# Making the low part of a streamed weight chunk two chunks ahead instead of three

## What is computed

```python
# block 1, two layers: modulated norms, FFN, attention, FFN
x = x + 0.5 * g1[:, None] * swiglu(h, ff_w13[l, 0], ff_w2[l, 0])
y = hybrid_conv_mla(...) if l % 2 == 0 else nsa_attention(...)
x = x + g2[:, None] * y
x = x + 0.5 * g3[:, None] * swiglu(h, ff_w13[l, 1], ff_w2[l, 1])
def swiglu(h, w13, w2):
    a, b = jnp.split(h @ w13, 2, axis=-1)
    return (jax.nn.silu(a) * b) @ w2
```

## Time and profile before

| | |
|---|---|
| Median of 3 runs | 3031.98 us (3030.12 to 3038.22) |
| The profiled execution | 3027.24 us |
| Its span, first to last instruction | 3025.4 us |
| Mean granted TensorE clock | 0.994 of full |
| TensorE busy | 2954.8 us, 98% |
| VectorE busy | 2338.3 us, 77% |
| ScalarE busy | 1727.1 us, 57% |
| GpSimd busy | 73.8 us, 2% |
| HBM | 243 GB/s over the span |

### The profile page before, as it was taken

The page is one execution under the profiler, slowest core; times in us unless marked ns, Lnnn a source line. Parts: engine busy times, 40 slices in busy tenths (PEclk is TensorE's granted clock), DMA queues, the critical chain, the costliest instruction groups (busy, mean ns, idle before and its releaser), DMA issues.

```text
span 3025.4 us, 56656 instructions
## 1 busy us (share of the span) xinstructions
PE 2954.8 (98%) x24887; PEld 2900.5 (96%) x24887; DVE 2338.3 (77%) x2648; ACT 1727.1 (57%) x1926; POOL 73.8 (2%) x143
## 2 busy tenths in 40 slices
PE   9999999999999999899999999999999999999999
PEld 8999999999989998899989999999999999899999
DVE  6897788888657567665777898898898898766776
ACT  5445454544535445444656777777777777545454
POOL 0110001010000000000000000000000000000000
PEclk9999999999999999999999999999999999999999
DMA  8885468687513653255416998998999899533352
GB/s 343 301 331 203 154 236 321 224 307 277 188 70 136 224 189 114 84 196 195 168 42 250 372 365 338 372 365 338 372 364 373 340 365 374 192 139 127 146 189 98
DMA packets 112412, 739.78 MB, mean 245 GB/s; under 512 B 12481, under 2 KB 12481, under 8 KB 32161
## 3 DMA queue, kind: packets, MB, share of 16 engines
q1 hardware_dynamic: 92304, 662.77, 58.4%
q0 software_dynamic: 19856, 73.34, 6.6%
HBM read 735.01 MB, written 1.05 MB: 243 GB/s over the span
## 4 chain that ended last, share of the span: by engine, by line
PE 84%; DVE 10%; ACT 4%; issue 1%; DMA 1%; SPq 0%; DVEq 0%; POOL 0%; ACTq 0%
PE ps L612 49%; PE ps L613 33%; DVE low L3079 3%; PE ps L627 2%; DVE AF L3061 2%; ACT whi L2081 2%; DVE att L3070 1%; DVE hl L3052 1%; DVE T L3052 1%; DVE gf L3064 1%; ACT cv L2066 0%; DVE T L3061 0%; DVE AF L3052 0%; DMA ring<-in_r 0%; ACT AF L2066 0%
## 5 line engine op out<-in xcount | busy, mean ns | idle before, releaser
L3079 DVE TENSOR_TENSOR low<-ring,whi 128x2048 fp32r<-128x2048 f32 x620 | 1414.3, 2290 | 369.9 <-ACT whi L2081 367.0
L2081 ACT ACTIVATE whi<-ring 128x2048 fp32r<-128x2048 f32 x620 | 1184.4, 1914 | 278.1 <-issue 173.6
L612 PE MATMUL ps<-whi,AR 128*128 128x256 f32 x5376 | 938.7, 278 | 0.0
L612 PEld LDWEIGHTS ps<-whi,AR 128*128 128x128 f32 x5376 | 819.0, 188 | 0.0
L612 PE MATMUL ps<-low,AR 128*128 128x256 f32 x2688 | 745.4, 277 | 0.0
L613 PE MATMUL ps<-hh,whi 128*128 128x256 f32 x2272 | 636.3, 280 | 0.2 <-DVE hl L3052 0.2
L613 PE MATMUL ps<-hl,whi 128*128 128x256 f32 x2272 | 629.1, 277 | 0.0
L613 PE MATMUL ps<-hh,low 128*128 128x256 f32 x2272 | 629.1, 277 | 0.0
L612 PEld LDWEIGHTS ps<-low,AR 128*128 128x128 f32 x2688 | 504.9, 188 | 0.0
L613 PEld LDWEIGHTS ps<-hh,whi 128*128 128x128 f32 x2272 | 426.1, 188 | 5.1 <-issue 1.0
L613 PEld LDWEIGHTS ps<-hl,whi 128*128 128x128 f32 x2272 | 426.0, 187 | 1.3 <-issue 1.0
(11 more groups left out here) (281 smaller groups left out, 3596.8 us busy)
## 6 DMA issues: line engine op xcount, KB each, us to landing
ring<-in_w SPq DMA_DIRECT2D x620, 1024.0 KB, 5.1
rring<-in_r POOLq DMA_DIRECT2D x135, 512.0 KB, 5.7
first<-in_r SPq DMA_DIRECT2D x8, 512.0 KB, 18.2
ring<-in_r SPq DMA_DIRECT2D x4, 512.0 KB, 8.6
rring<-in_r SPq DMA_DIRECT2D x3, 512.0 KB, 17.3
AF<-in_mem SPq DMA_DIRECT2D x1, 1024.0 KB, 8.4
X<-in_x SPq DMA_DIRECT2D x1, 1024.0 KB, 16.2
AF<-in_cst POOLq DMA_DIRECT2D x1, 1024.0 KB, 5.9
```

Source lines behind the costliest of these rows:

```text
L612: return self.e.matmul(out, l, r, start=start, stop=stop, skip_group_check=True)
L2081: self.e.activation(N.whi[:, c % HB, :], N.slot(c), ACT.Copy).then_inc(N.sem["hi"], 1)
L3079: self.e.tensor_tensor(N.wlo(c), N.slot(c), N.whi[:, c % HB, :].bitcast(F32), ALU.subtract).then_inc(N.sem["lo"], 1)
```

## The change

VectorE's `chunk()` makes lows up to two chunks ahead of its count instead of three. ScalarE's `chunk()` stays at three, as do the four places above that make lows with numbers of their own, and the number of buffers.

```diff
--- before.py
+++ after.py
@@ -3081,7 +3081,7 @@
             self.count.tick("lo", ())
 
     def chunk(self):
-        self.split_to(self.chunks + HB - 1)
+        self.split_to(self.chunks + HB - 2)
         self.chunks += 1
 
     def start(self):
```

## The result

Before 3031.74 us (median of 7 runs, 3026.75 to 3038.22), after 3041.90 us (7 runs, 3035.46 to 3044.78). The ratio of all runs is 1.0026, 95% interval 1.0013 to 1.0038: the change costs 7.9 us of 3032, between 3.9 and 11.5. (The two medians alone are 10.2 us apart, 1.0034.) That is about the 0.3% named as the bound of "same": the ratio is under it, its interval reaches over it. The median is inside the range of 3017 to 3048, and 0.9 above the narrower 3024 to 3041. It is not nothing: the forecast was +0.25.

A forecast was written before the change was run, and what follows sets the result against it. TensorE, busy 98% of the span, was taken to bound the kernel. Losses of +17.7 and gains of -17.45 gave net +0.25 us on the runs' median: 3032.2 us, range 3017 to 3048 (forecast alone 3024 to 3041).

The forecast's parts named there:

- Loss 1: ff(0,1) to ff(1,0): low 85 made behind the fold, TensorE stands 8.3 us; 7.05 late plus 1.7 clock, +8.75.
- Loss 2: ff2 to conv layer: 6.9 late plus 1.7 clock, less 4.9 and 1.0 absorbed in the conv layer, +2.7 us.
- Loss 3: Other starts: hybrid +0.9, NSA +1.85, fox +0.65, ff3 +2.4, end of hybrid +0.4; together +6.2 us.
- Experts: Expert stage: lows late only at four even-to-odd expert borders, 0.2 us taken for each, +0.8 in all.
- Conv `out_proj`: Conv layer's `out_proj`: a low 0.35 us late, but a `finish` one low shorter closes a gap of 1.1; -0.75.
- Gains: Attention: TensorE gaps behind waiting lows close; hybrid 4.95, NSA 3.9, fox 5.0, MoBA 2.6, cross 0.98; -17.45 us.
- rival A: Slower: attention gaps stay, as ScalarE stands between; gains 6 instead of 17.45, net +11.7, 3043.7 us; chance 0.18.
- Rival D: Half clock lasts 10.2 us behind both 8-us stalls: +6.8, 3039 us; chance 0.49 together with the forecast and E.
- Rival C: Faster: smaller losses, gains 20; last condition, fold one low (2.29) earlier in both `finish`es: -12.7, 3019.3 us; chance 0.24.
- E: Nothing happens: lows keep their times, no stalls or closings show, 3032 us; chance 0.49 with the forecast and Rival D.

The follow-up runs named there:

- experiment 5: `starts_warm`: `two_starts_alone` plus 60 dummy TensorE matmuls ahead of the wait for the two lows at both starts; span 3043.4 against 3043.3 us, one execution.
- `attention_alone`: Kernel before, with two ahead only at listed calls inside the five attention stages, three elsewhere; 3014.15 us, ratio 0.9941 to the kernel before.
- `two_starts_alone`: Experiment 2: kernel before, with two ahead only at the calls of chunks 82 and 210, moving lows 85 and 213; 3053.03 us, ratio 1.0069.
- `starts_fixed`: Changed kernel, plus one line making the low of the chunk after the FFN before `finish`; 3011.97 us, ratio 0.9934 to the kernel before.
- `best`: `starts_fixed` with three ahead again from chunk 587 on (ff3); 3009.83 us, ratio 0.9936 to the kernel before.
- `best_b`: `best` run again, side by side with a rerun of `starts_fixed`; 3011.56 us, ratio 0.9936 to the kernel before.
- `after`: The changed kernel itself, two ahead at all of VectorE's `chunk()` calls, against the kernel before; median 3041.90 us, first trace's span 3043.0.
- `inner_alone`: Kernel before, with two ahead only in the steady FFN parts and the experts, three elsewhere; 3032.53 us against 3030.92, ratio 1.0013.

## Why the prediction came out as it did

The range held, and the ratio of 1.0026 is within the 0.3% that the forecast called no change. Of the working, most terms held and one step failed. That the sum came so near is in part luck, as several terms missed in both directions.

- **Loss 1, right.** +8.75 against 9.6 and 9.4. The wait is 8.15 against the 8.3 worked out; the clock cost 2.6 (experiment 5) against 1.7, as more than 3.4 us of half clock fell on matmuls: 5.4 in the first trace.
- **Loss 2, the step that failed:** "VectorE sets the pace of this layer", from which 5.9 of 8.6 were to be given back. Nothing was (-0.3). The raw stall was right, +8.4 to 9.3.
- **Loss 3, right in place, small in size.** Hybrid to the decimal, NSA 2.1 to 2.5 for 1.85. Fox 2.3 and 0.8 for 0.65: in the first trace alone 3.4 us at 0.50 stand behind its wait (1134.3 to 1137.7). ff3 4.6 for 2.4: the wait was 4.18 (not 3.1), since `low` 593 ended at 2888.54 behind `conv3`, gate and its split, and 1.4 followed behind it, where 3.4 us were granted 0.50 (2888.7 to 2892.1). The forecast had no clock in this term. Its 0.7 for a shorter `finish` came as 0.6, at chunk 586, and stands in the row of cross attention.
- **Experts: no wait for `low`, as predicted.** The +0.8 itself can't be told from nothing: +0.2, -1.0 and +0.6 in three traces with two ahead, -0.8, -0.7 and +1.2 in three with three ahead there (`attention_alone`, `two_starts_alone`, `starts_warm`).
- **Conv `out_proj`, +0.9 for -0.75.** Most of it lies in chunk 222, and there the time goes with the length of the half clock near 1600: 3.4 us in the trace before, 6.8 (two times 3.4) and 10.2 in those of the changed kernel. At 10.2 us a trace with two ahead has +0.8 at this chunk and the two with three ahead +2.2 and +2.3; so the predicted gain may be there and be hidden. That is not settled.
- **Gains, right in kind, in part right by luck.** The sums for hybrid, MoBA and cross are within 0.3, but for 1.6 at chunks 43 to 45 in one trace (half clock again, 3.4 us that this trace does not have). But not all the gaps named for them closed. Hybrid's 1.14, before and in the changed kernel:

```profile
340.28 0.36 PE L612 MATMUL ps<-hh,whi 128*128 128x256 f32 x1 [1.14 <-DVE hl L3052]
```

```profile
338.74 0.36 PE L612 MATMUL ps<-hh,whi 128*128 128x256 f32 x1 [1.14 <-DVE hl L3052]
```

  The row comes out by 4.0 at chunk 45, for 3.8 counted there, and 0.7 in small pieces. Fox's 0.68 stayed too (0.63), its 2.42 left 0.39. Cross closed 0.6 and 0.4 of its 0.98 and owes the rest of its row to the 0.6 of `finish` named above.

  In NSA 6.5 stand for 3.9: at chunk 121 a recorded gap of 0.53 gave 1.5 in every kernel with two ahead. In fox 3.7, and 1.45 more at chunks 165 to 167 (taken back in the first trace by the half clock at 1134.3), are together the 5.0. What is left of the table's -8.2 and -1.7, about 1.6 each at chunk 130 and at 163, is the clock's, and not the change's for sure. At 130 the trace before has 3.4 us at 0.50 from 927.0 on and the changed kernel's have none. At 163 it has the 10.2 us of the earlier trace rows, and theirs are 3.4. Both gains are also in `starts_warm` (-1.5 at the next chunk, -1.1), which has three ahead there, and one or the other is missing from a trace with two ahead (0.0 and -0.2).
- **The sum.** In both traces the conv layer lost 5.6 that the forecast had given back, ff3 2.2 and chunk 219 to 223 1.7 more than forecast; NSA and chunk 163 gained 6 more, of which some 3 is clock. The rest differs from trace to trace. The forecast was near because these in good part cancel.

**Why the conv layer gave nothing back.** VectorE in that layer in the changed kernel, against the earlier trace rows, and TensorE at the gap of the earlier trace rows. The first line is of the trace before, the others of the changed kernel:

```profile
1510.78 0.74 DVE L3070 TENSOR_REDUCE att<-ps 128x1 f32<-128x256 f32 x2
```

```profile
1494.52 2.29 DVE L3079 TENSOR_TENSOR low<-ring,whi 128x2048 fp32r<-128x2048 f32 x1 [1.92 <-ACT whi L2081]
...
1498.62 0.88 DVE L3061 SCALAR_TENSOR_TENSOR AF<-ps,sm,gs 128x256 f32<-128x256 f32 x2 [1.81 <-ACT gs L2066]
...
1506.93 0.88 DVE L3061 SCALAR_TENSOR_TENSOR AF<-ps,sm,gs 128x256 f32<-128x256 f32 x2 [1.44 <-ACT gs L2066]
...
1525.79 0.76 DVE L3070 TENSOR_REDUCE att<-ps 128x1 f32<-128x256 f32 x2 [3.78 <-PE ps L613]
```

```profile
1543.13 0.58 PE L613 MATMUL ps<-warm 128*128 128x256 f32 x1 [4.92 <-DVE gf L3064]
```

The wait of 4.91 for `whi` is gone as predicted. In its place VectorE waits 1.81 and 1.44 for ScalarE's `gs`, and 3.78 for TensorE's scores before the reduce `att`. I had read back from TensorE's gap of 4.86 through VectorE's queue to the 4.91, and passed over this reduce, which in the trace before had just no wait in front of it. In this trace TensorE was 6.0 us late against the trace before at chunk 211 and 15.3 at chunk 214. VectorE had made up 4 of this by its `low` at 1518.93 (1507.79 in the trace before), but at the reduce it waited for TensorE's scores and was 15.0 late again. `starts_fixed` says it from the other side: it saves the same wait, without the late start, and has -0.3 over chunks 214 to 219; its VectorE stands 3.24 us at the same reduce. `two_starts_alone`, which saves no wait there, has -0.3 too. So the saved wait was worth nothing there in either case, which is shown; the prediction took it as slack at the bottleneck.

By its number rival A (3043.7) is nearest to the 3041.90, but its mechanism isn't seen: more than 17 us of gains came. Rival D had the clock: the half clock did last 10.2 us behind the first stall, as D said, but half of it fell into the wait, so the drops cost 4.2 in all against 3.4 in the forecast and 10.2 in D. Rival C's last condition is not seen either: the fold comes at 561.89 for 563.09, the 1.2 us by which this trace was ahead, and not one `low` earlier. Nor is E: the stalls are there.

## What to carry to other kernels

How far ahead a helper engine works is a number per place, not per kernel: two is better where the helper's queue has urgent work behind the waiting instruction, three is needed where a step has no call of its own, as at the end of an FFN. Before a lead is shortened, list the places where calls are skipped or where a consumer takes two at once; here two lows of 620, each made one call later, cost 21 us by themselves (experiment 2). And a saved wait on a path is a gain only if the next instruction that waits for somebody else on that path isn't due yet: follow the queue to that instruction, also where the trace shows it with no wait.

## What the runs showed of the hardware

**Two paces of TensorE at the same granted clock.** Busy time by stretch over eight chunks of ff2, `best` and then `best_b`, the same program:

```profile
1312.00:1355.50 43.50, 43.50 (x387) 43.50 (x385) 21.11 (x14) 18.33 (x15) 0.00 (x0) 1.00 0.54 194
```

```profile
1326.50:1371.70 45.20, 45.20 (x386) 45.20 (x385) 19.66 (x14) 18.35 (x14) 0.00 (x0) 1.00 0.52 186
```

Both are 100% busy at 1.00, with 387 and 386 matmuls in 43.5 and in 45.2 us. A chunk of 48 takes 5.44 or 5.65 us; over ff2 the difference is 6.4 us. It was there in 3 of the 11 traces that have two or three chunks of lead (`after`, `starts_fixed`, `best_b`), and in two (`starts_fixed`, `best`) for chunks 6 to 10, in ff(0,0), until the first chunk with other matmuls in it, which took it back to 5.44. In ff2 such a chunk (6.09 against 5.91) did not end it. In all three the time from chunk 180's first matmul to that of chunk 181, just ahead of the slow part, was 12.61 us, in the others 12.29 or 12.50, so it shows already at the start of the stage. What sets it is open; no run here tried to. That the change has no part in it isn't shown: the three are among the seven traces with two ahead in ff2, and none of the four with three ahead has it there, which chance alone would give about once in five times. Against it, traces with three ahead have the same 5.65 in shorter stretches elsewhere: `attention_alone` at chunks 216 and 217, and it and three others at 589 and 590. So some of the 7.9 us may be this pace. It is the largest difference between two traces of one kernel here, and nearly the size of the effect of this change, so traces have to be compared stage by stage and not by their spans.

**The clock's drop.** Behind idle of 8.15 and 7.20 us on TensorE (`two_starts_alone`) the half clock went on for 3.4 us and part of the next stretch; with dummy matmuls through the wait it stayed at 1.00. The Trainium skill (TensorE: Matmul & The Clock Gate, "Why this matters for your kernels") advises against such gaps, and the runs agree: 4.2 us for two of them.

The same idle does not always bring the same drop. The gap of 2.04 us at chunk 128 stands in five traces: in `attention_alone`, `two_starts_alone` and `starts_warm` 3.4 us at 0.50 follow and the chunk takes 1.7 longer, in the trace before and in `inner_alone` the clock stays at 1.00. At chunk 163 the half clock lasts 10.2 us in five traces, 6.8 in three and 3.4 in three, and the chunk is within 0.3 of the trace before with 10.2, 1.1 to 1.3 shorter with 6.8, and 1.7 to 1.8 shorter with 3.4. Kernels with two and with three ahead are among those with 10.2 and with 6.8. What decides it is open.
